# Two-layer encoder on one core: the ninth expert pass begins ahead of its branch, and the last result is computed in halves

## What is computed

```python
def moe_swiglu(h, router_w, w1, w3, w2):
    logits = (xf @ router_w).astype(jnp.float32)
    top_val, top_idx = lax.top_k(logits, TOP_K)
    gates = jax.nn.softmax(top_val, axis=-1)
    ...
    def expert_block(args):
        tok_b, e = args
        return swiglu(x_pad[tok_b], w1[e], w3[e], w2[e])
    ...
    y = y.reshape(P, D) * buf_g[:, None].astype(y.dtype)
    out = jax.ops.segment_sum(y, buf_tok, num_segments=N + 1)[:N]
...
x = x + gate2 * y
```

## Time and profile before

| | us |
|---|---|
| median of 3 runs | 1699.55 |
| lowest, highest of them | 1698.03, 1702.09 |
| the profiled execution | 1705.27 |
| its span, from the first to the last instruction | 1703.3 |
| PE busy, share of the span | 1656.0, 97% |
| DVE busy | 1359.5, 80% |
| ACT busy | 1111.5, 65% |

### The profile page before, as it was taken

The page is one execution under the profiler, slowest core; times in us unless marked ns, Lnnn a source line. Parts: engine busy times, 40 slices in busy tenths (PEclk is TensorE's granted clock), DMA queues, the critical chain, the costliest instruction groups (busy, mean ns, idle before and its releaser), DMA issues.

```text
span 1703.3 us, 20715 instructions
## 1 busy us (share of the span) xinstructions
PE 1656.0 (97%) x8278; PEld 1371.2 (81%) x8278; DVE 1359.5 (80%) x1571; ACT 1111.5 (65%) x1367; POOL 77.0 (5%) x49
## 2 busy tenths in 40 slices
PE   6998999999999999999999999999999999998997
PEld 3865899997688788888888888888887888886885
DVE  2383787895423899899998999998998998997995
ACT  3365444342323678788887888887887887885883
POOL 0000000000000000200200200200201101000000
PEclk8999999999999999999999999999999999998998
DMA  9934678787623499899999899999999998996990
GB/s 353 367 105 171 227 291 303 259 310 279 216 99 148 183 341 371 334 362 376 355 374 359 335 373 380 352 366 350 353 367 346 356 380 321 357 355 260 375 353 27
DMA packets 169711, 518.95 MB, mean 305 GB/s; under 512 B 6765, under 2 KB 8954, under 8 KB 169610
## 3 DMA queue, kind: packets, MB, share of 16 engines
q1 hardware_dynamic: 156704, 473.32, 74.4%
q10 hardware_dynamic: 12906, 44.25, 6.9%
HBM read 516.50 MB, written 1.05 MB: 304 GB/s over the span
## 4 chain that ended last, share of the span: by engine, by line
PE 90%; DVE 5%; ACT 2%; DMA 1%; issue 1%; POOL 0%; ACTq 0%; DVEq 0%
PE bank L1126 19%; PE bank L1130 19%; PE bank L1129 19%; PE bank L669 8%; PE bank L663 3%; PE bank L854 2%; PE bank L856 2%; PE bank L855 2%; DVE w_lo L1971 2%; PE bank L1140 2%; PE bank L807 2%; PE bank L1062 1%; PE bank L874 1%; PE bank L872 1%; PE bank L875 1%; PE bank L642 1%
## 5 line engine op out<-in xcount | busy, mean ns | idle before, releaser
L1971 DVE TENSOR_TENSOR w_lo<-ring,w_hi 128x1024 fp32r<-128x1024 f32 x756 | 915.0, 1241 | 78.6 <-ACT w_hi L1442 55.6
L1442 ACT ACTIVATE w_hi<-ring 128x1024 fp32r<-128x1024 f32 x756 | 794.3, 1062 | 206.7 <-PE bank L1130 204.8
L1126 PE MATMUL bank<-w_hi,hg_hi 128*128 128x512 f32 x1008 | 396.9, 394 | 3.9 <-DVE w_lo L1971 3.9
L1129 PE MATMUL bank<-w_lo,hg_hi 128*128 128x512 f32 x1008 | 394.1, 391 | 0.0
L1130 PE MATMUL bank<-w_hi,hg_lo 128*128 128x512 f32 x1008 | 393.9, 391 | 0.0
L1126 PEld LDWEIGHTS bank<-w_hi,hg_hi 128*128 128x128 f32 x1008 | 190.4, 189 | 47.8 <-DVE w_lo L1971 7.7
L1130 PEld LDWEIGHTS bank<-w_hi,hg_lo 128*128 128x128 f32 x1008 | 190.3, 189 | 39.9
L1129 PEld LDWEIGHTS bank<-w_lo,hg_hi 128*128 128x128 f32 x1008 | 190.5, 189 | 38.8
L1126 PE MATMUL bank<-w_hi,hid_hi 128*128 128x512 f32 x504 | 198.8, 394 | 0.0
L1130 PE MATMUL bank<-w_hi,hid_lo 128*128 128x512 f32 x504 | 196.5, 390 | 0.0
L1129 PE MATMUL bank<-w_lo,hid_hi 128*128 128x512 f32 x504 | 196.3, 389 | 0.0
(11 more groups left out here) (290 smaller groups left out, 1709.3 us busy)
## 6 DMA issues: line engine op xcount, KB each, us to landing
ring<-in_moe_w SPq DMA_DIRECT2D x168, 2048.0 KB, 7.9
ring<-in_ada_w SPq DMA_DIRECT2D x24, 2048.0 KB, 12.7
ring<-in_moe_w ACTq DMA_DIRECT2D x21, 2048.0 KB, 8.1
ring<-in_ffn_w SPq DMA_DIRECT2D x15, 2048.0 KB, 8.8
ring<-in_da_w_in SPq DMA_DIRECT2D x6, 2048.0 KB, 20.3
ring<-in_gla_w_in SPq DMA_DIRECT2D x6, 2048.0 KB, 13.0
ring<-in_da_w_out SPq DMA_DIRECT2D x2, 2048.0 KB, 8.5
ring<-in_gla_w_out SPq DMA_DIRECT2D x2, 2048.0 KB, 8.5
```

The source lines that it names most:

```text
L1126: begun = mm(out[:, :], xhi, whi[:, cs], start=first, stop=False)
L1129: mm(out[:, :], xhi, wlo[:, cs], start=False, stop=False)
L1442: A(w_hi[:, Q % PIECES, :], raw_piece(m, q), ACT.Copy).then_inc(hi_done, 1)
L1971: v.tensor_tensor(w_lo[:, Q % PIECES, :], raw_piece(m, q), w_hi[:, Q % PIECES, :].bitcast(F32), ALU.subtract).then_inc(lo_done, 1)
```

## The change

- **The first twelve pieces of pass 8 stand ahead of the branch.** `expert(m)` gets bounds `q0, q1`. Pieces 0 to 11 (`HEAD = SPREAD_AT + 5` = 12) of pass 8 now run in every case, and the branch stands between pieces 11 and 12. ACT and DVE may make pieces of pass 8 while pass 7 still runs (`m_end`).
- **The result of pass 7 is handled inside pass 8**, as those of passes 0 to 6 are in the pass behind them. POOL adds it.
- **SP stores the output early**, once POOL has added the eighth result; this is the whole output where no overflow pass runs. Where one runs, ACT stores it again at the end.
- **The last result goes by halves** (`high_end`, `out_end`, `spread_end`, `store_end`): the steps of the chain wait for 512 columns each, the first half is spread into banks 4 and 5 and the second into 2 and 3, and ACT stores 256 KB behind each of the four adds. The branch on the second overflow pass stands ahead of this chain on all three engines.
- **`SPREAD_AT` goes from 5 to 7** in every pass, and `take_spread` with it, to q = 8 to 11.
- **PE's three register loads** move from behind pass 7 to between passes 6 and 7.

```diff
--- before.py
+++ after.py
@@ -109,7 +109,8 @@
     g_last = {g: PPC * i + PPC - 1 for g, i in last_slot.items()}
...
     TURN_AT = {g_last["w3", c] + (2 if c else 4): c for c in range(ECH)}
-    SPREAD_AT = 5
+    SPREAD_AT = 7
+    HEAD = SPREAD_AT + 5
     PT_AT = g_last["w3", 0] + 5
...
     GATHER_AT = g_last["w3", ECH - 1] + 5
...
@@ -529,7 +535,7 @@
                     src, k, n = expert_source(m, i)
...
 
-            sp.wait_ge(s_fin, 1)
+            sp.wait_ge(s_add, 4 * NE)
             for tt in range(TT):
...
             sp.wait_ge(s_out, 16 * TT)
@@ -570,7 +576,7 @@
             nc.gpsimd.affine_select(out=lower_e, in_=lower_e, compare_op=ALU.is_gt, fill=0.0, base=0,
...
             pool.wait_ge(s_xa, 4)
-            for m in range(1, NE):
+            for m in range(1, NE + 1):
                 for n in range(4):
...
                     dst = x_acc[:, tt, half * 512:(half + 1) * 512]
@@ -1082,9 +1088,9 @@
                               start=(tt == 0), stop=(tt == TT - 1))
...
 
-            def expert(m):
-                for q in range(EQ):
+            def expert(m, q0=0, q1=EQ):
+                for q in range(q0, q1):
                     i, p = divmod(q, PPC)
...
                     Q = piece_no(m, q)
@@ -1140,7 +1146,7 @@
                             last = nc.tensor.transpose(psum[4 + j // 4][:, j % 4 * P:(j % 4 + 1) * P],
...
                         last.then_inc(s_et, 1)
-                    if q == SPREAD_AT and 0 < m < NE:
+                    if q == SPREAD_AT and 0 < m <= NE:
                         spread(m)
...
                         slots_turned(m)
@@ -1154,23 +1160,36 @@
                         gather(group_in[m], False)
...
                         gather(group_in[m], True)
-                if m >= NE - 1:
-                    spread(m + 1)
+            def spread_end():
+                for half in range(2):
+                    pe.wait_ge(s_eye_end, half + 1)
+                    for tt in range(TT):
+                        to, own = PmT[:, tt * P:(tt + 1) * P], slice(half * 512, (half + 1) * 512)
+                        out = psum[4 - 2 * half + tt]
+                        mm(out[:, :], to, hid_1[0][:, 0, own], start=True, stop=False)
+                        mm(out[:, :], to, hid_1[1][:, 0, own], start=False, stop=True).then_inc(s_sct_end, 1)
 
...
             keep_pace(1, 2)
-            for m in range(NE):
+            for m in range(NE - 1):
                 expert(m)
...
             more = [pe.value_load(ovi[0:1, o:o + 1], min_val=1, max_val=2) for o in range(OVER)]
+            expert(NE - 1)
+            expert(NE, 0, HEAD)
             with pe.If(more[0] == 2):
-                expert(NE)
+                expert(NE, HEAD, EQ)
                 with pe.If(more[1] == 2):
+                    spread(NE + 1)
                     expert(NE + 1)
                     with pe.If(more[2] == 2):
+                        spread(NE + 2)
                         expert(NE + 2)
+                spread_end()
 
...
         @block.scalar
@@ -1491,19 +1510,36 @@
                 src, k, n = expert_source(e, i)
...
 
-            def expert(m, over=None):
-                m_end = max(m, NE - 1)
+            def high_end():
+                act.wait_ge(s_gge, NE + 1)
+                for half in range(2):
+                    own = slice(half * 512, (half + 1) * 512)
+                    act.wait_ge(s_yt_end, half + 1)
+                    A(hid_1[0][:, 0, own], y_raw[:, own], ACT.Copy, scale=gcol[:, 0:1]).then_inc(s_yh_end, 1)
+            def store_end():
+                for half in range(2):
+                    own = slice(half * 512, (half + 1) * 512)
+                    for tt in range(TT):
+                        act.wait_ge(s_add_end, 2 * half + tt + 1)
+                        act.dma_start(t["out"][0, tt * P:(tt + 1) * P, own], x_acc[:, tt, own]).then_inc(s_out_end, 16)
+                act.wait_ge(s_out_end, 16 * 2 * TT)
+            def expert(m, over=None, q0=0, q1=EQ):
+                m_end = max(m, NE)
                 if m > NE:
...
                 split_to(piece_no(m, AHEAD - 1), m_end)
-                for q in range(EQ):
+                for q in range(q0, q1):
                     i, p = divmod(q, PPC)
                     what, c, part = eorder[i]
-                    if q == 2 and 0 < m < NE:
+                    if q == 2 and 0 < m <= NE:
                         high_out(m - 1)
-                    if 0 <= q - SPREAD_AT - 1 < 4 and 0 < m < NE:
+                    if 0 <= q - SPREAD_AT - 1 < 4 and 0 < m <= NE:
                         take_spread(m, q - SPREAD_AT - 1)
...
                     if q == g_first["w3", c] and what == "w3":
@@ -1536,8 +1572,6 @@
                         load_over(over[m - NE], m, q // PPC - 1 + SLOTS)
...
                     load_over(over[0], NE, SLOTS - 1)
-                if m >= NE - 1:
-                    high_out(m)
 
...
             for m in range(NE - 1):
@@ -1546,13 +1580,18 @@
             more = [act.value_load(ovi[0:1, o:o + 1], min_val=1, max_val=2) for o in range(OVER)]
...
             expert(NE - 1, over)
+            expert(NE, over, 0, HEAD)
             with act.If(more[0] == 2):
-                expert(NE, over)
+                expert(NE, over, HEAD, EQ)
                 with act.If(more[1] == 2):
+                    high_out(NE)
                     expert(NE + 1, over)
                     with act.If(more[2] == 2):
+                        high_out(NE + 1)
                         expert(NE + 2, over)
-            for i in range(SLOTS):
+                high_end()
+                store_end()
+            for i in range(SLOTS + (HEAD - 2) // PPC):
                 wait_landed(act, ring_slot(NE, i))
...
         @block.vector
@@ -1996,20 +2035,54 @@
                                                   hid_1[0][:, 0, own].bitcast(F32), ALU.mult, ALU.subtract)
...
 
-            def expert(m, over=None):
+            def out_serial(m):
+                raw_out(m)
+                low_out(m)
+                if m == NE:
+                    dve.wait_ge(s_add, 4 * NE)
+                    dve.wait_ge(s_out, 16 * TT)
...
+            def out_end():
+                dve.wait_ge(w_free, PIECES + piece_no(NE, EQ))
+                for half in range(2):
+                    own = slice(half * 512, (half + 1) * 512)
+                    v.tensor_tensor(y_raw[:, own], psum[2 + half][:, :], g2bc[:, own], ALU.mult).then_inc(s_yt_end, 1)
+                for half in range(2):
+                    own = slice(half * 512, (half + 1) * 512)
+                    dve.wait_ge(s_yh_end, half + 1)
+                    v.scalar_tensor_tensor(hid_1[1][:, 0, own], y_raw[:, own], gcol[:, 0:1],
+                                           hid_1[0][:, 0, own].bitcast(F32), ALU.mult,
+                                           ALU.subtract).then_inc(s_eye_end, 1)
+                dve.wait_ge(s_add, 4 * NE)
+                dve.wait_ge(s_out, 16 * TT)
+                for half in range(2):
+                    for tt in range(TT):
+                        dve.wait_ge(s_sct_end, 2 * half + tt + 1)
+                        dst = x_acc[:, tt, half * 512:(half + 1) * 512]
+                        v.tensor_tensor(dst, dst, psum[4 - 2 * half + tt][:, :], ALU.add).then_inc(s_add_end, 1)
+            def expert(m, over=None, q0=0, q1=EQ):
 
...
 
-                m_end = max(m, NE - 1)
+                m_end = max(m, NE)
                 split_to(piece_no(m, AHEAD - 1), m_end)
-                for q in range(EQ):
+                for q in range(q0, q1):
                     i, p = divmod(q, PPC)
                     what, c, part = eorder[i]
-                    if q == 0 and 0 < m < NE:
+                    if q == 0 and 0 < m <= NE:
                         raw_out(m - 1)
-                    if q == 3 and 0 < m < NE:
+                    if q == 3 and 0 < m <= NE:
                         low_out(m - 1)
...
                     if q == g_last["w3", c] and what == "w3":
@@ -2039,17 +2112,8 @@
                         overflow_table()
...
                         gathered(group_in[m])
-                if m >= NE - 1:
-                    raw_out(m)
-                    low_out(m)
-                    if m == NE - 1:
-                        dve.wait_ge(s_add, 4 * (NE - 1))
-                    for n in range(4):
-                        tt, half = divmod(n, 2)
-                        dve.wait_ge(s_sct, 4 * m + n + 1)
-                        dst = x_acc[:, tt, half * 512:(half + 1) * 512]
-                        v.tensor_tensor(dst, dst, psum[2 + n][:, :], ALU.add).then_inc(s_scb, 1)
-                    dve.wait_ge(s_scb, 4 * (m + 1))
+                if m > NE:
+                    dve.wait_ge(w_free, PIECES + piece_no(m, EQ))
 
...
             gathered(0)
@@ -2060,13 +2124,16 @@
             over = [dve.value_load(ovi[0:1, OVER + o:OVER + o + 1], min_val=0, max_val=NE - 1) for o in range(OVER)]
...
             expert(NE - 1, over)
```

(23 more changed lines are left out.)

## The result

The changed kernel takes 1683.13 us (median of 4 runs, 1680.33 to 1684.03) beside 1700.82 us for the kernel before (4 runs, 1698.03 to 1706.01). The ratio is 0.9886, with a 95% interval of 0.9864 to 0.9909: 1.1% faster, 19.4 us by the ratio (15.5 to 23.1). Four later runs of it gave a median of 1681.50 us and a ratio of 0.9884 (0.9867 to 0.99). The forecast was 1680.2 us in a range of 1676.0 to 1685.0.

A forecast was written before the change was run, and what follows sets the result against it. PE was taken as the bound at 1.37 us a piece, DVE a tenth behind. Savings of 11.2 + 1.0 + 7.2 = 19.4 us took the median from 1699.55 to 1680.2 us, range 1676.0 to 1685.0.

The forecast's parts named there:

- Between passes 7 and 8: From pass 7's last matmul into pass 8: PE's waits and low clock vanish, 11.2 us saved.
- the two things costed at nothing: In pass 8: ACT issuing the loads and SP's early 1 MB store, both taken to cost no time.
- The branch: Inside pass 8: all three engines fall into the branch's body, so it costs nothing.
- The rival of a fetch at an entered branch: Inside pass 8: PE stops up to 2.93 us at the branch, later matmuls may slow; 1685.7 us, chance 0.06.
- PE's loads and the later spread: Around passes 6 and 7: moved register loads and later spread together save 1.0 us, between 3.4 saved and 2.15 lost.
- The reasoning for the loads: While PE loads registers, ACT and DVE catch up, so the loads replace PE's waits rather than add to them.
- PE would wait at piece 7 of pass 6 in place of the spread: Pass 6: PE comes to piece 7 earlier and waits there, so only part of each wait is won.
- In passes 1 to 5 there is nothing to win: The later spread saves nothing in passes 1 to 5, where PE was read to wait once, for 0.4 us.
- The end: Behind pass 8's last matmul: halves, stores behind each add and the jump moved ahead end the span 7.2 us earlier.
- The rival of the low clock: At the end: the clock falls in PE's pause, last add at T + 6.7, 1.1 us more, 1681.3 us; chance 0.20.
- The jump: The branch past unrun overflow passes, at most 2.93 us on DVE, now stands ahead of the last chain, in idle time.
- The sum: Over the whole kernel: 11.2 + 1.0 + 7.2 = 19.4 us saved, giving 1680.2 us, 1.1% less.

The follow-up runs named there:

- e1: The changed kernel with every spread behind piece 5 again, the twelve pieces ahead of the branch kept: 1685.02 us, ratio 0.9904 to the kernel before.
- e4: The changed kernel without SP's early store of the output in pass 8 and DVE's wait for it: 1682.43 us, ratio 0.9889 to the kernel before.
- e5: The changed kernel with the branch at the very start of pass 8, no piece ahead of it: 1683.19 us, ratio 0.9897 to the kernel before.
- e6: The changed kernel with PE loading its three register values three times over (nine loads) between passes 6 and 7: 1683.27 us, ratio 0.9891 to the kernel before.
- e10: The changed kernel with DVE's and ACT's six register loads each placed singly, one every four pieces, in passes 5 and 6: 1678.72 us, ratio 0.9868 to the kernel before.

## Why the prediction was right, step by step

- **Between passes 7 and 8: 11.2 us forecast.** Passes 7 and 8 together got 11.7 us shorter. By e1, 0.4 and 0.2 of this belong to the later spread; 11.1 are left. The term was right. Of the two things costed at nothing, SP's store cost nothing by e4; ACT's issues of the loads have no run of their own, but PE has no wait in the whole of pass 8.
- **The branch: nothing forecast, nothing found.** PE's matmuls on its two sides start 0.23 us apart, and it costs the same ahead of piece 0 (e5). The rival of a fetch at an entered branch fell.
- **PE's loads and the later spread: 1.0 us forecast.** The reasoning for the loads (ACT and DVE catch up) is what e6 shows, but it wasn't needed: three loads cost PE nothing at all (e10). That PE would wait at piece 7 of pass 6 in place of the spread came true (0.54 us at 1310.70). For the spread the step "In passes 1 to 5 there is nothing to win" failed. There were 0.2 us a pass, 1.0 in all, which no idle time shows, because the holes are shorter than the modelled tail of a matmul. (The single wait of 0.4 us that the forecast read from the earlier trace rows lies in pass 0, at 618 us; in passes 1 to 5 none is printed. The sum doesn't use it.) In passes 6 and 7, where the forecast looked, 0.9 came. In all 2.1 us by e1.
- **The end: 7.2 us forecast, 6.3 measured.** The rival of the low clock, given 0.20, is what the profile shows: the last add at 6.65 us behind the last piece (6.7 in the rival, 5.6 in the forecast) and a first matmul at 2.36 (2.17). From the last add to the end it took 3.0 us where 3.15 were forecast. Of the 0.9 us that are missing the clock is 0.7: with it held, e1 and e6 end 0.7 us sooner. The other 0.2 is missing in e1 and e6 as well, where the first spread matmul also starts 0.2 us later than forecast. Taking the clock at its upper level was the mistake; that it was a toss show the two of seven profiles in which it held.
- **The jump** was hidden on all three engines, as forecast: DVE passes its branch at 1665.58, 5.5 us ahead of its gate multiply, and ACT's and PE's first steps behind it start 0.1 us behind the end of what they wait for.
- **The sum: 19.4 us** forecast, 19.4 by the ratio, and 19.5 between the profiles from pass 1 on. That they agree so well is partly luck: the end's 0.9 us too few and the spread's 1.1 us too many cancel. The median came out at 1683.13 us rather than 1680.2. The medians of before and after (17.7 us apart) move by a microsecond or more with the runs in them: that of before went from 1699.55 to 1700.82 us by one run more, and that of the changed kernel was 1681.50 us in the later set.

## What to carry to other kernels

When a result's chain stands bare between two stretches of matmuls, put its steps among the pieces of the next stretch, and where a run-time branch stands between them, run a part of that stretch ahead of it, knowing what it costs where the branch isn't taken (8.1 us here). By e5 the pieces ahead of the branch are not what wins the time; they only serve the case without the pass, and keeping the bare chain for that case alone, on the other side of the branch, was not tried. Keep jumps past unused code and rows of register loads off the engines that feed the bound one: placing twelve loads singly won 3.9 us by the profiles, a fifth of the whole change, for a few lines. Compare the distances between starts, not the printed idle time, where losses are small and repeat.

## What the runs showed of the hardware that was not expected

- A row of register loads on DVE or ACT costs PE more than its printed waits: 2.44 us of waits were 3.9 us of time. On PE three cost nothing, nine a pause of 2.05 us.
- Holes of 0.07 to 0.11 us between matmuls of 0.23 show in no idle time, and made 0.2 us a pass.
- Without an overflow pass, the adds of POOL (about 2 us each) rather than the twelve pieces set the end.
- A jump past unused passes took 2.9 to 3.1 us from DVE's last add to the store's issue, whether it passed two or three of them. A branch that is entered left PE's matmuls 0.23 us apart.
- Beside an add of POOL a split of DVE takes up to 2.3 us instead of 1.22: in the changed kernel all 32 splits from pass 1 on that took over 1.3 us overlap such an add. At the start of pass 8 of the changed kernel four in a row, from 1560.37, took 2.0 to 2.3 us. The wait at 1325.37 above stands right behind such a split too (1322.99, 2.33 us).
